# A hybrid decoder block on eight cores: one edit in six parts, from the banks of the attention values to the last multiply

## The chip, the cores and the metric

The kernel runs on all 8 cores of one Trainium2 chip. Each core has one of the 8 batch elements and runs the same program on it, with no exchange between cores. The metric is the device time in microseconds (us) of the slowest core. A core has five engines: PE (TensorE, matrix multiply), DVE (VectorE), ACT (ScalarE), POOL (GpSimd) and SP (SyncE). SP issues most DMAs here and POOL the rest; both run their instructions strictly in order, as the three others do.

## The reference

```python
h = rms_norm(x, norm_mix_pre)                       # (B, 2048, 1024)
u_a, v_a, q, k, v_b, g_a, g_b = split(h @ w_in)     # 7 x 1024 columns
# branch A: chunks of 128 tokens, 8 groups of 128 channels
y_a = gelu(u_a) * (tril(W_s) @ layer_norm(gelu(v_a)) + b_s)
# branch B: 16 heads of 64, three (window, dilation) patterns
for window, dilation in ((128, 1), (512, 4), (2048, 16)):
    o_p, lse_p = causal attention of t on t - j*dilation, j <= window//dilation, ALiBi bias
y_b = sum_p softmax_p(lse_p) * o_p
merged = sigmoid(g_a + b0) * (y_a @ w_a_proj) + sigmoid(g_b + b1) * (y_b @ w_b_proj)
x = x + rms_norm(merged @ w_out, norm_mix_post)
f = square(relu(rms_norm(x, norm_ffn_pre) @ w_ff1)) @ w_ff2      # 1024 -> 4096 -> 1024
x = x + rms_norm(f, norm_ffn_post)
```

## The kernel before

The program is one list of operations, each with the buffers and PSUM banks that it reads and writes. A planner (`Plan.schedule`) gives each operation a cost, and always takes the ready operation of lowest `prio` on the engine that is free first; from that comes a fixed order for every engine. `Plan.emit` writes it out with semaphore waits. So a changed number moves many instructions, and at run time each engine stands at the head of its list until that instruction's waits are met.

The stages, in order of time:

1. **Start.** x is loaded, normed, transposed to `hT`, with the projections of the first heads between.
2. **Attention**, in 8 pairs of heads (`hp` 0 to 7). For a pair, `proj_qk` makes Q and K (8 groups of 8 matmuls of 512 columns, from the pair's weights `wqk`), casts them out of banks 6 and 7 on DVE, and makes two more orders of K: `KT0` by a copy on DVE (L560), `KT1` by a copy on ACT (L562). `s_job` makes scores in banks 0 to 3, ACT takes the exponential to `Et` (L654), DVE multiplies by the bias table to `PT` (L666); there are 8 such jobs of the first pattern and 12 of the others. `pv_class` has four classes `c` in each pair: it gathers all three patterns of a quarter of the tokens, for both heads, in banks 4 and 5, 48 matmuls that alternate between the heads. Then come the logarithm of the sums (L725, ACT, twice), the exponential of that (L727, ACT) and two products into `ybT` (L730, DVE), which free the banks for the next class. The Q and K groups of a pair, and the value projection of pairs of pairs (`proj_v`), stand between the scores and values of the pairs ahead of it, and keep PE at work while it would wait for ACT.
3. **V_A**: 16 tiles of `hT` by `wva`, each in two groups of 8 matmuls. The first 7 (`NRAW`) are made during the last pairs and copied raw (`raw`, L832) because gelu waits for the last exponential of attention (`lastexp`); they alternate in banks 6 and 7. The copies `hTc` are made on POOL (L821).
4. **U**, 8 groups `g` of four (L887 takes gelu), and the **gate products** (`name="gate"`, 4 to a group g, each 4 matmuls of 128 columns), which read all layer-normed V_A tiles `gc` (L852), and which DVE turns into `yaT` (L900, L904). The gate products of group g have the priority of U's group g + 4.
5. **Merge**: for each of 8 blocks and 4 windows four groups (`g0`, `g1` on `hT`, `g3` on `ybT`, `g2` on `yaT`).
6. **Output projection** of 16 token tiles, with norms, the new x stored to `x1_scr`, and `h2T`. The feed-forward layers follow in two halves `s`, each with 7 products in place of 8 (sums and differences of weight blocks, `w1_comb` and `w2_comb`, are made earlier on DVE and stored). The first `NMIX` = 8 groups of half 0's first layer are mixed among the output projections; they use banks 0 and 1 alone. The others take bank pairs in rotation. Their weights come into a ring of 5 buffers (`rslot`; the mixed ones use four of them).
7. **End.** When the 7 products of the second layer are gathered, `fin` makes the factor of each token tile on POOL (L1215, L1217), and DVE multiplies by factor and gain (L1223) and adds x (L1225), half a tile at a time.

The weights of the last pair have a buffer of their own, `wqk2`, on the first 4 KB of `stg[0]`, the staged values of pairs 4 and 5: classes 0 and 1 of pair 5 are the last to read that part. Loads of `wqk` are issued on POOL.

## Time and profile before

| | |
|---|---|
| median of 3 runs | 1166.86 us (lowest 1165.67) |
| the profiled execution | 1166.27 us |
| its slowest core, first to last instruction | 1164.7 us (the eight: 1158.1 to 1164.7) |
| PE busy | 1119.2 us, 96% of the span |
| DVE, ACT, POOL busy | 735.7, 529.0, 149.2 us |
| mean granted TensorE clock | 0.987 |

The profile is of the slowest core. PE's ends are modelled, so one matmul of 512 columns shows about 380 ns though the next one starts 217 ns after it; cadence is to be read from starts. "Busy" PE time thus covers all but true stops. The granted clock is given per stretch, as a share of full speed: 1.00 is 2.4 GHz and 0.50 is 1.2 GHz.

### The profile page before, as it was taken

How to read it: one execution, taken by the hardware profiler on the slowest of the kernel's cores; microseconds unless marked ns; L12 is line 12 of the kernel's file. 1: busy time of each engine (PE TensorE's matmuls, PEld its weight loads, DVE VectorE, ACT ScalarE, POOL GpSimd, SP SyncE). 2: the span in 40 equal slices, each digit the busy share in tenths (PEclk: the TensorE clock that was granted, in tenths of full speed). 3: DMA queues.
4: the chain of work that ended last, by engine and by line, in shares of the span. 5: the costliest groups of instructions: out<-in, count | busy, mean ns of one | idle time of the engine just before them, and what ended most of it. 6: DMA issues, size and time to landing. Idle time of an engine off the chain costs nothing.

```text
span 1164.7 us, 20926 instructions; the slowest of 8 cores (1158.1 to 1164.7 us)
## 1 busy us (share of the span) xinstructions
PE 1119.2 (96%) x7348; PEld 569.9 (49%) x7348; DVE 735.7 (63%) x1224; ACT 529.0 (45%) x771; POOL 149.2 (13%) x260
## 2 busy tenths in 40 slices
PE   8899999997989999999999999999999999999996
PEld 3666665664545445444444444444444444444442
DVE  5867777776777644755444466985783157774417
ACT  4567887787776863021221135653321124432021
POOL 3300000001122441000000012520000031000002
PEclk9899999998999999899999999999999999999999
DMA  8776756676442439389887779975457459547433
GB/s 222 191 180 124 149 117 148 121 146 136 106 69 63 73 63 147 46 179 234 228 215 193 191 250 280 292 255 162 148 170 255 149 182 310 173 155 264 145 113 141
DMA packets 95337, 197.57 MB, mean 170 GB/s; under 512 B 39169, under 2 KB 55681, under 8 KB 90370
## 3 DMA queue, kind: packets, MB, share of 16 engines
q1 hardware_dynamic: 86082, 154.28, 42.6%
q0 software_dynamic: 9152, 41.95, 21.6%
q8 instruction: 61, 1.00, 0.4%
q14 instruction: 42, 0.34, 0.1%
HBM read 194.11 MB, written 56.62 MB: 215 GB/s over the span
## 4 chain that ended last, share of the span: by engine, by line
PE 85%; issue 4%; DVE 4%; ACT 3%; DMA 3%; POOL 1%; DVEq 0%; SPq 0%; ACTq 0%; POOLq 0%
PE pst L195 85%; DMA sb_xt<-x 2%; ACT sb_Et L654 1%; PE pst L199 1%; DVE sb_ybT L730 1%; DMA sb_r<-w_comb 1%; ACT sb_gc L852 0%; DVE sb_PT L666 0%; ACT sb_Lr L725 0%; POOL sb_st L1020 0%; ACT sb_junk L1022 0%; DVE sb_yaT L904 0%; ACT sb_gv L833 0%; ACT sb_Lr L727 0%; DVE sb_tmpm L900 0%
## 5 line engine op out<-in xcount | busy, mean ns | idle before, releaser
L654 ACT ACTIVATE sb_Et<-pst 128x1024 bf16<-128x1024 f32 (+1 forms) x160 | 151.0, 975 | 31.9 <-PE pst L195 16.7
L195 PE MATMUL pst<-sb_r,sb_hid 128*128 128x512 bf16 x640 | 139.4, 379 | 0.3 <-DVE sb_hid L1129 0.3
L666 DVE TENSOR_TENSOR sb_PT<-sb_Et,sb_EB 128x1024 bf16<-128x1024 bf16 (+2 forms) x200 | 110.1, 569 | 36.9 <-ACT sb_Et L654 25.1
L195 PE MATMUL pst<-sb_hT,sb_wqk 128*128 128x512 bf16 x512 | 122.3, 386 | 3.8 <-DVE sb_hT L516 3.1
L965 ACT ACTIVATE sb_sg<-pst,sb_small 128x512 f32<-128x512 f32 x64 | 44.0, 687 | 176.2 <-PE pst L195 71.0
L195 PE MATMUL pst<-sb_merged,sb_r 128*128 128x512 bf16 x512 | 122.2, 379 | 0.5 <-DVE sb_hid L1121 0.5
L195 PE MATMUL pst<-sb_hT,sb_wg 128*128 128x512 bf16 x512 | 116.2, 379 | 0.0
L195 PEld LDWEIGHTS pst<-sb_r,sb_hid 128*128 128x128 bf16 x640 | 62.5, 98 | 76.0 <-issue 0.7
L195 PE MATMUL pst<-sb_TB,sb_r 128*128 128x512 bf16 x384 | 94.1, 379 | 2.8 <-ACT sb_sne L1118 1.7
L195 PEld LDWEIGHTS pst<-sb_merged,sb_r 128*128 128x128 bf16 x512 | 49.8, 98 | 61.1 <-issue 1.8
L195 PEld LDWEIGHTS pst<-sb_hT,sb_wg 128*128 128x128 bf16 x512 | 49.9, 98 | 59.0
L195 PEld LDWEIGHTS pst<-sb_hT,sb_wqk 128*128 128x128 bf16 x512 | 46.9, 99 | 61.2 <-issue 14.6
L1118 ACT ACTIVATE sb_sn<-pst 128x512 f32<-128x512 f32 x72 | 43.0, 597 | 72.6 <-PE pst L195 72.6
L969 DVE SCALAR_TENSOR_TENSOR sb_sg<-sb_sg,pst 128x512 f32<-128x512 f32 x32 | 22.0, 687 | 84.5 <-PE pst L195 84.5
L1205 DVE TENSOR_TENSOR sb_sn<-pst,sb_sn 128x512 f32<-128x512 f32 x24 | 16.4, 690 | 87.6 <-ACT sb_sn L1202 49.5
L195 PE MATMUL pst<-sb_PT,sb_V 128*128 128x64 bf16 (+3 forms) x1280 | 65.0, 209 | 1.5 <-DVE sb_ybT L730 1.4
L195 PE MATMUL pst<-sb_QT,sb_KT 64*128 64x256 bf16 (+1 forms) x768 | 52.5, 250 | 12.7 <-ACT sb_Et L654 12.2
L195 PE MATMUL pst<-sb_ybT,sb_wg 128*128 128x512 bf16 x256 | 62.2, 387 | 1.8 <-DVE sb_tmpm L900 1.8
L195 PEld LDWEIGHTS pst<-sb_PT,sb_V 128*128 128x128 bf16 x1280 | 56.0, 100 | 12.7 <-issue 5.8
L195 PE MATMUL pst<-sb_yaT,sb_wg 128*128 128x512 bf16 x256 | 61.3, 384 | 0.0
L195 PE MATMUL pst<-sb_wout,sb_merged 128*128 128x512 bf16 x256 | 58.5, 379 | 2.5 <-DVE sb_tp L1030 2.5
L195 PEld LDWEIGHTS pst<-sb_TB,sb_r 128*128 128x128 bf16 x384 | 37.2, 98 | 48.2 <-issue 4.4
(123 smaller groups left out, 1668.1 us busy)
## 6 DMA issues: line engine op xcount, KB each, us to landing
w_bf<-w POOLq DMA_DIRECT2D x32, 512.0 KB, 7.8
sb_PB<-w_bf SPq DMA_DIRECT2D x32, 512.0 KB, 8.8
w_comb<-sb_PB SPq DMA_DIRECT2D x32, 512.0 KB, 9.6
sb_r<-w_comb SPq DMA_DIRECT2D x32, 512.0 KB, 4.6
sb_r<-w_comb SPq DMA_DIRECT2D x16, 1024.0 KB, 5.1
sb_r<-w_bf SPq DMA_DIRECT2D x32, 384.0 KB, 3.8
sb_r<-w_bf SPq DMA_DIRECT2D x12, 1024.0 KB, 5.7
...
```

The lines of the kernel that those rows point to most:

```text
L195: e.matmul(out, lhsT=l, rhs=r, start=st, stop=sp, skip_group_check=True))
L199: fns = [lambda e, a=a, b=b: e.transpose(out=a, in_=b, identity=ident) for a, b in outs_ins]
L654: P.act(lambda e: e.activation(out=et[:, :, 0:W], in_=psall[:, sb:sb + 2, 0:W], func=AF.Exp, scale=0.125), 2 * W, [], [et.key()], [sb, sb ...
L666: P.dve(lambda e: e.tensor_tensor(out=o, in0=i0, in1=i1, op=ALU.mult), n, rk, [pt.key()], rate=2, name="mask")
L730: P.dve(lambda e, hh=hh, lo=lo: e.tensor_tensor(out=ybT[lo:lo + 64, hp, 512 * c:512 * c + 512], in0=psr(bks[hh], lo, lo + 64), in1=lr[lo:l ...
L965: P.act(lambda e, j=j, cb=cb, pj=pj, s_=s_: e.activation(out=s_[j][:], in_=pj, func=AF.Tanh, scale=0.5, bias=small[:, bg_c + 8 * j + cb:bg ...
L969: P.dve(lambda e, pj=pj, s_=s_: e.scalar_tensor_tensor(out=s_[1][:], in0=s_[1][:], scalar=1.0, in1=pj, op0=ALU.add, op1=ALU.mult), 512, [s ...
L1118: P.act(lambda e: e.activation(out=o[:], in_=ps(bk), func=AF.Copy), 512, [], [o.key()], [bk], name="snap")
L1205: P.dve(lambda e: e.tensor_tensor(out=d[:], in0=ps(bk), in1=d[:], op=ALU.add), 512, [d.key()], [d.key()], [bk])
```

## The change

Six parts:

1. **PV on three banks.** For pairs 6 and 7 the two heads of a class are written one after the other and no longer alternate, and each takes the next of banks 4, 5 and 7 in turn. The last class still has banks 0 and 1. For that, the raw V_A groups use bank 6 alone.
2. **A home for the last weights.** `wqk2` moves from 64 KB to 60 KB, on the part of `ybT` that pair 7 writes, and its load is placed when pair 5 starts, behind the last class of pair 4. `hTc`'s first four buffers change their order.
3. **K copies on GpSimd.** The 32 copies to `KT1` move from ACT to POOL.
4. **Gate products** of group g get the priority of U's group g + 2.
5. **Six mixed groups** (`NMIX` = 6). The next two of half 0 become groups like the rest; the ring's rule changes with the number.
6. **Final weights ahead of the factor.** `gfin` is multiplied in as soon as a half is gathered and squared, and the factor and the addition of x become one instruction.

```diff
-    wqk.append(buf("wqk2", 64 * K, [8, 256]))
+    wqk.append(buf("wqk2", 60 * K, [8, 256]))
...
-                    c1 = P.act(lambda e, o1=o1, s=s: e.activation(out=o1, in_=s, func=AF.Copy), 512, [kk],
-                               [KT1[d].key((512 * w, 512 * w + 512))])
+                    c1 = P.pool(lambda e, o1=o1, s=s: e.tensor_copy(out=o1, in_=s), 1.2, [kk], [KT1[d].key((512 * w, 512 * w + 512))])
...
-        bks = (0, 1) if hp == NHP - 1 and c == 3 else (4, 5)
+        bks = (4, 5)
+        if hp >= 6:
+            r = [(4, 5, 7)[(pctr3[0] + j) % 3] for j in range(2)]
+            pctr3[0] += 2
+            bks = tuple(r)
+        if hp == NHP - 1 and c == 3:
+            bks = (0, 1)
...
-        for j in range(8):
+        for hs in (((0,), (1,)) if hp >= 6 else ((0, 1),)):
+            bk = [bks[hh] for hh in hs]
+            for j in range(8):
...
-                for hh in range(2):
+                    for hh in hs:
...
-            P.pe(mms, [V0[d].key(), p0t[j].key()], bks, name="pv0")
+                P.pe(mms, [V0[d].key(), p0t[j].key()], bk, name="pv0")
...
-            elif hp == NHP - 2:
-                load_wqk(hp + 1, b0 - 30)
+            elif hp == NHP - 3:
+                load_wqk(hp + 2, b0 - 5, anchor[0])
...
-    hTc = [buf(f"hTc{i}", o * K, [8, 128]) for i, o in enumerate((68, 70, 92, 104, 160, 64, 66, 198, 200, 202))]
+    hTc = [buf(f"hTc{i}", o * K, [8, 128]) for i, o in enumerate((64, 66, 68, 70, 92, 104, 160, 198, 200, 202))]
...
     def vbanks(n):
+        if n < NRAW:
+            return (6, 6)
         return {NRAW: (2, 3)}.get(n, (6, 7))
...
-            P.prio = U0 + 10 * (g + 4) + 5 + n4
+            P.prio = U0 + 10 * (g + 2) + 5 + n4
...
-    NMIX = 8
+    NMIX = 6
...
-                        P.dve(lambda e, src=src, hs=hs: e.scalar_tensor_tensor(out=src, in0=src, scalar=sp_[:, c0 + 3:c0 + 4], in1=gfin[:, hs],
-                                                                              op0=ALU.mult, op1=ALU.mult), 512, [rk, gfin.key()] + k, k, bks)
-                        P.dve(lambda e, src=src, hf=hf, xh=xh: e.tensor_tensor(out=xh(hf), in0=src, in1=xh(hf), op=ALU.add), 512,
-                              [kh[hf]] + k, [kh[hf]], bks)
+                        P.dve(lambda e, src=src, hf=hf, xh=xh: e.scalar_tensor_tensor(out=xh(hf), in0=src, scalar=sp_[:, c0 + 3:c0 + 4], in1=xh(hf),
+                                                                                      op0=ALU.mult, op1=ALU.add), 512, [rk, kh[hf]] + k, [kh[hf]], bks)
...
+                def gain(src, hf, k, bks=()):
+                    P.dve(lambda e: e.tensor_tensor(out=src, in0=src, in1=gfin[:, 512 * hf:512 * hf + 512], op=ALU.mult), 512, k + [gfin.key()], k, bks)
...
                 elif o == 6:
                     acc(u2[p], bk)
                     sq(u2[p][:], 9, [u2[p].key()], [])
+                    gain(u2[p][:], 1, [u2[p].key()])
                     fin(8 * s + p, [(s1[p][:], [s1[p].key()], []), (u2[p][:], [u2[p].key()], [])], 8)
```

Where this moves instructions, three places follow.

PE's list in pair 5, from the last products of class 0 on (`sb_QT_55` is the Q of pair 5, `sb_stgV_48` ends a class, `sb_wqk_64` is `wqk2`). Before:

```order
L195 MATMUL pst<-sb_PT_2_80,sb_stgV_48 128x128 x8
L195 MATMUL pst<-sb_QT_55,sb_KT_57 128x128 x8
L195 MATMUL pst<-sb_QT_55,sb_KT_1_61 128x256 x6
L195 MATMUL pst<-sb_QT_55,sb_KT_1_61 128x128 x2
L195 MATMUL pst<-sb_QT_55,sb_KT_57 128x128 x8
```

and now:

```order
L195 MATMUL pst<-sb_QT_55,sb_KT_57 128x128 x8
L195 MATMUL pst<-sb_PT_2_80,sb_stgV_48 128x128 x8
L195 MATMUL pst<-sb_hT,sb_wqk_64 128x512 x8
L195 MATMUL pst<-sb_QT_55,sb_KT_1_61 128x256 x6
L195 MATMUL pst<-sb_QT_55,sb_KT_1_61 128x128 x2
L195 MATMUL pst<-sb_hT,sb_wqk_64 128x512 x8
L195 MATMUL pst<-sb_QT_55,sb_KT_57 128x128 x8
L195 MATMUL pst<-sb_hT,sb_wqk_64 128x512 x8
```

Q and K of the last pair have moved from pairs 5 (end) and 6 wholly into pair 5. Pair 6 then has 2 groups of V_A as its only other work and pair 7 has 8, where before the V_A groups that stood among both were 12, beside 5 projections.

PE's list at the end of V_A (`sb_wva`), where U (`sb_wu`) and the gate products (`sb_wsT`) follow. Before:

```order
L195 MATMUL pst<-sb_wva,sb_hTc_139 128x512 x16
L195 MATMUL pst<-sb_hT,sb_wu_112 128x512 x16
L195 MATMUL pst<-sb_hT,sb_wu_113 128x512 x24
L195 MATMUL pst<-sb_wsT,sb_gc 128x16x8 x8
L195 MATMUL pst<-sb_hT,sb_wu_114 128x512 x8
```

and now:

```order
L195 MATMUL pst<-sb_wva,sb_hTc_139 128x512 x16
L195 MATMUL pst<-sb_hT,sb_wu_110 128x512 x16
L195 MATMUL pst<-sb_wsT,sb_gc 128x16x8 x8
L195 MATMUL pst<-sb_hT,sb_wu_112 128x512 x8
L195 MATMUL pst<-sb_wsT,sb_gc 128x16x8 x8
```

Two U groups and not five lie between the last V_A group and the first gate products, and 12 gate products and not 20 are left when U ends.

DVE's list at the very end, from the gathering of the last two tiles. Before:

```order
L1205 TENSOR_TENSOR sb_sn_205<-pst,sb_sn_205 128x512
L1205 TENSOR_TENSOR sb_sn_206<-pst,sb_sn_206 128x512
L1223 SCALAR_TENSOR_TENSOR sb_sn_201<-sb_sn_201,sb_st_183,sb_gfin 128x512
L1223 SCALAR_TENSOR_TENSOR sb_sn_205<-sb_sn_205,sb_st_183,sb_gfin 128x512
L1225 TENSOR_TENSOR sb_hx<-sb_sn_201,sb_hx 128x512
L1225 TENSOR_TENSOR sb_hx<-sb_sn_205,sb_hx 128x512
L1223 SCALAR_TENSOR_TENSOR sb_sn_202<-sb_sn_202,sb_st_184,sb_gfin 128x512
L1223 SCALAR_TENSOR_TENSOR sb_sn_206<-sb_sn_206,sb_st_184,sb_gfin 128x512
L1225 TENSOR_TENSOR sb_hx<-sb_sn_202,sb_hx 128x512
L1225 TENSOR_TENSOR sb_hx<-sb_sn_206,sb_hx 128x512
```

and now:

```order
L1242 TENSOR_TENSOR sb_sn_205<-sb_sn_205,sb_gfin 128x512
L1215 TENSOR_TENSOR sb_sn_206<-pst,sb_sn_206 128x512
L1233 SCALAR_TENSOR_TENSOR sb_hx<-sb_sn_201,sb_st_183,sb_hx 128x512
L1233 SCALAR_TENSOR_TENSOR sb_hx<-sb_sn_205,sb_st_183,sb_hx 128x512
L1242 TENSOR_TENSOR sb_sn_206<-sb_sn_206,sb_gfin 128x512
L1233 SCALAR_TENSOR_TENSOR sb_hx<-sb_sn_202,sb_st_184,sb_hx 128x512
L1233 SCALAR_TENSOR_TENSOR sb_hx<-sb_sn_206,sb_st_184,sb_hx 128x512
```

Behind the last gathering (L1215) 5 instructions are left and not 8, and two behind the last factor and not four. In POOL's list the K copies stand between DMA issues: a copy waits there for whatever the issue ahead of it waits for.

## Rows read from the trace of the kernel before

**Rows 1.** Stretches: busy of PE, PEld, DVE, ACT, POOL; granted clock; DMA share; GB/s

```profile
200.00:276.00 76.00, 74.36 (x844) 47.77 (x841) 58.00 (x101) 61.32 (x74) 5.23 (x10) 1.00 0.62 128
276.00:296.00 20.00, 13.11 (x159) 9.59 (x160) 9.83 (x18) 13.19 (x19) 3.08 (x5) 0.74 0.57 119
296.00:325.00 29.00, 27.95 (x254) 14.32 (x253) 22.45 (x38) 24.18 (x28) 3.24 (x4) 1.00 0.49 103
325.00:342.00 17.00, 12.34 (x196) 8.62 (x195) 11.01 (x17) 11.37 (x16) 4.22 (x5) 1.00 0.38 64
...
484.00:492.00 8.00, 5.10 (x21) 1.94 (x20) 4.82 (x10) 0.69 (x1) 0.00 (x0) 0.67 0.00 0
...
777.00:800.00 23.00, 19.85 (x100) 8.50 (x99) 14.02 (x21) 11.66 (x20) 2.22 (x6) 1.00 0.58 189
```

**Rows 2.** PE in order of time: start, us, instructions, idle before and its releaser

```profile
276.35 0.61 PE L195 MATMUL pst<-sb_PT,sb_stgV 128*128 128x128 bf16 x8 [0.46 <-DVE sb_PT L666]
...
279.45 0.34 PE L195 MATMUL pst<-sb_QT,sb_KT 64*128 64x256 bf16 x4 [1.89 <-ACT sb_Et L654]
...
281.57 3.10 PE L195 MATMUL pst<-sb_PT,sb_V 128*128 128x64 bf16 x40 [0.28 <-DVE sb_ybT L730]
...
295.31 3.70 PE L195 MATMUL pst<-sb_hT,sb_wqk 128*128 128x512 bf16 x16
...
338.65 1.85 PE L195 MATMUL pst<-sb_PT,sb_V 128*128 128x64 bf16 x40 [0.20 <-DVE sb_ybT L730]
```

**Rows 3.** POOL in order of time at the load of the last weights

```profile
286.02 0.54 POOL L476 DMA_DIRECT2D sb_wqk<-w_qk  x1 [10.99 <-PE pst L195]
```

**Rows 4.** ACT's groups in 60 to 270 us: busy, mean ns, idle before

```profile
L654 ACT ACTIVATE sb_Et<-pst 128x1024 bf16<-128x1024 f32 x82 | 83.1, 1032 | 20.7 <-PE pst L195 12.8 <-DVE sb_ybT L730 4.0 <-DVE sb_PT L666 3.1
L562 ACT ACTIVATE sb_KT<-sb_KT 128x512 bf16<-128x512 bf16 x25 | 33.8, 1364 | 9.3 <-DVE sb_KT L555 9.3
L725 ACT ACTIVATE sb_Lr<-pst 64x512 f32<-64x512 f32 x40 | 23.7, 592 | 14.4 <-PE pst L195 13.6
L727 ACT ACTIVATE sb_Lr<-sb_Lr 128x512 f32<-128x512 f32 x20 | 12.5, 626 | 0.3
```

**Rows 5.** Waits in 60 to 270 us: total, times, longest

```profile
PE pst L195 <- ACT sb_Et L654: 1.9, 8, 0.5
```

**Rows 6.** POOL's copies of hT: ns min/median/max, first and last start

```profile
L821 POOL COPY sb_hTc<-sb_hT x16: 1026/1044/2019, 287.1 to 422.0; 128x1024 bf16<-128x1024 bf16 x16
```

**Rows 7.** DVE and POOL in order of time at 317 us

```profile
318.49 1.13 DVE L666 TENSOR_TENSOR sb_PT<-sb_Et,sb_EB 128x1024 bf16<-128x1024 bf16 x1 [0.31 <-ACT sb_Et L654]
...
317.00 2.08 POOL L821 COPY sb_hTc<-sb_hT 128x1024 bf16<-128x1024 bf16 x2 [12.26 <-PE pst L195]
```

**Rows 8.** DVE's groups in 60 to 270 us

```profile
L666 DVE TENSOR_TENSOR sb_PT<-sb_Et,sb_EB 128x1024 bf16<-128x1024 bf16 x81 | 54.8, 691 | 14.9 <-ACT sb_Et L654 10.9 <-PE pst L195 2.9
```

**Rows 9.** ACT at the end of V_A, then PE where yaT is waited for

```profile
432.62 0.60 ACT L837 ACTIVATE sb_gv<-pst 128x512 f32<-128x512 f32 x1 [0.98 <-PE pst L195]
...
436.56 1.23 ACT L852 ACTIVATE sb_gc<-sb_gv,sb_bst 128x1024 bf16<-128x1024 f32 x1
...
487.77 3.57 PE L195 MATMUL pst<-sb_ybT,sb_wg 128*128 128x512 bf16 x8 [1.80 <-DVE sb_tmpm L900]
```

**Rows 10.** The end: PE, DVE, then two steps of the chain of waits

```profile
1127.70 26.71 PE L195 MATMUL pst<-sb_r,sb_hid 128*128 128x512 bf16 x123
...
1154.23 1.28 DVE L1205 TENSOR_TENSOR sb_sn<-pst,sb_sn 128x512 f32<-128x512 f32 x2
1157.02 1.42 DVE L1223 SCALAR_TENSOR_TENSOR sb_sn<-sb_sn,sb_st,sb_gfin 128x512 f32<-128x512 f32 x2 [1.50 <-POOL sb_st L1217]
...
1160.88 1.29 DVE L1225 TENSOR_TENSOR sb_hx<-sb_sn,sb_hx 128x512 f32<-128x512 f32 x2
...
1155.02 0.73 ACT sb_junk L1208 x2
...
1156.35 0.57 POOL sb_st L1217
```

More of the change, by code:

```diff
@@ L610, in build_nc @@
     anchor = [None]
+    pctr3 = [0]
     sctr, p0ctr, p12ctr, ectr, lctr = [0], [0], [0], [0], [0]
@@ L705, in pv_class @@
-        for n2 in range(2):
-            mms = []
-            for m in (2 * n2, 2 * n2 + 1):
-                w = 64 if m < 3 else 32
-                for hh in range(2):
-                    r = p1t[n2][:, hh, 256 * (m % 2):256 * (m % 2) + 4 * w]
-                    mms.append((out(hh, 0, 4, 32 * m, w), lhs(V1[d], 4 * c + m, hh), r.rearrange("p (a m) -> p a m", a=4), False, False,
-                                4 * w, False))
-            P.pe(mms, [V1[d].key(), p1t[n2].key()], bks, name="pv1")
@@ L714, in pv_class @@
[L714 to L719 removed]
+        for hs in (((0,), (1,)) if hp >= 6 else ((0, 1),)):
+            bk = [bks[hh] for hh in hs]
+            for j in range(8):
+                mms = []
+                for blk in (2 * j, 2 * j + 1):
+                    w = 16 if blk < 15 else 8
+                    for hh in hs:
+                        r = p0t[j][:, hh, 256 * (blk % 2) + 4 * w * c:256 * (blk % 2) + 4 * w * c + 4 * w]
+                        mms.append((out(hh, 0, 4, 8 * blk, w), lhs(V0[d], blk, hh), r.rearrange("p (a m) -> p a m", a=4), first[hh], False,
+                                    4 * w, False))
+                        first[hh] = False
+                P.pe(mms, [V0[d].key(), p0t[j].key()], bk, name="pv0")
+            for n2 in range(2):
+                mms = []
+                for m in (2 * n2, 2 * n2 + 1):
+                    w = 64 if m < 3 else 32
+                    for hh in hs:
+                        r = p1t[n2][:, hh, 256 * (m % 2):256 * (m % 2) + 4 * w]
+                        mms.append((out(hh, 0, 4, 32 * m, w), lhs(V1[d], 4 * c + m, hh), r.rearrange("p (a m) -> p a m", a=4), False, False,
+                                    4 * w, False))
+                P.pe(mms, [V1[d].key(), p1t[n2].key()], bk, name="pv1")
+            mms = []
+            for a in range(4):
+                for hh in hs:
+                    mms.append((ps(bks[hh])[:, 128 * a:128 * a + 128], stg[sd][:, 4 * c + a, hj, 64 * hh:64 * hh + 128],
+                                p2t[:, hh, 128 * a:128 * a + 128], False, a == 3, 128, False))
+            anchor[0] = P.pe(mms, [stg[sd].key((4 * c, 4 * c + 4)), p2t.key()], bk, name="pv2")
@@ L1237, in build_nc @@
                     sq(s1[p][:], 8, [s1[p].key()], [])
+                    gain(s1[p][:], 0, [s1[p].key()])
                 elif o == 3:
```

14 lines of the change are left out of this document (2 added, 12 removed).

## The prediction

> **What bounds the kernel now.** The page says that PE is busy for 96% of the span, so I went first to the stretches in which it is not. The table of stretches [rows 1] shows where PE's share falls: 6.9 us idle of 20 from 276 to 296, 1.0 of 29 to 325, 4.7 of 17 to 342, 2.9 of 8 from 484 to 492 and 3.2 of 23 from 777 to 800. Add the end, in which PE has stopped, about 10 us after its last matmul at 1154.4 [rows 10]. The second thing in that table is the granted clock: 0.74 in the first of these stretches and 0.67 in the fourth. A matmul group shows both levels. 40 products of values take 3.10 us after the idle time at 281 and 1.85 us at 338 [rows 2]; 8 matmuls of 512 columns take 3.57 us at 487 [rows 9], where the usual pace is 26.71 / 123 = 0.217 us each, 1.74 us [rows 10]. So after a stop PE runs for a while at 1.2 GHz and not at 2.4. Everywhere else PE is full at clock 1.00, and there an edit can only lose. From 200 to 276 it is idle for 1.6 us in 76.
>
> So the prize is small and can be counted: about 13 us of idle and 3.4 us of slow clock (13.11 busy us at 0.74) around the last pairs, 4.6 us at 484, 3 us at 777, and some of the end.
>
> **Last weights and three banks.** Why does PE stop at 276? The projections of pair 7 are its filler, and their weights are issued only at 286.02, having waited for PE [rows 3], since their place was still read by pair 5; the first products follow at 295.31 [rows 2]. In between PE has only scores and values, and waits for ACT. With the new place the load can go behind pair 4's last class, a class, some 11 us, ahead of class 0 of pair 5, whose last values ended at 277.0 (276.35 + 0.61) [rows 2], so near 266. Load to first use was 9.3 us, so the weights are there by 275.5, and PE's new list wants them behind class 0 of pair 5, whose end that is. I count no wait for them, with 1.5 us to spare.
>
> But filler is moved, not made. All 8 groups (8 x 1.74 = 13.9 us) now stand in pair 5, and pair 6 has only 2 V_A groups. A class of pair 6 asks PE for 1.85 + 0.6 us of values and five score jobs of some 0.3 us [rows 2], 3.9 us, and 0.9 us of V_A. It asks ACT for five exponentials (1.03, the smaller ones less), two logarithms of 0.59 and one of 0.63 [rows 4], 6.7 us. With two banks a class cannot be faster than its own loop either: values, logarithms, exponential, two products, values again: 1.85 of values, 3 x 0.6 for ACT's steps [rows 4], and DVE's products of about that length with the hand-overs between, some 7 us at full clock (an estimate), and 1.25 more of values at slow clock [rows 2], 8.3. Three banks let the first head of a class start before the last class is cleared; ACT's 6.7 us stay. So in pair 6 PE idles 6.7 - 4.8 = 1.9 us a class, 7.6 us in all. Pair 7 has 8 V_A groups, 3.9 - 0.6 + 3.5 = 6.8 us of PE a class against some 4.8 of ACT (three exponentials), so PE is the longer; one bank for V_A makes each of its groups wait for a copy, for which I leave 3 us. Before: 12.6 + 3.4 = 16.0 us. Now: 7.6 + 3 = 10.6 us. **Gain 5 us.** Bounds: if pair 6 goes round in 8.3 us like the slow loop, 4 x 1.6 = 6.4 us more for the loop and some 1.6 of slow clock are lost, -3 us; if ACT's work spreads so that pair 6 has 2 us of idle, +11. I take 5, because the stretch from 325 to 342, at 73% busy, kept clock 1.00 and is the nearest thing to the new pair 6.
>
> **K copies.** On ACT a copy takes 1.36 us [rows 4], 32 x 1.36 = 44 us of ACT. But PE waited for an exponential only 1.9 us in 60 to 270 [rows 5], so off the path nearly all of it buys nothing there; in pairs 5 to 7 it is already counted, as my 6.7 us have no copy in them. POOL's price for this copy stands nowhere; a copy of twice the elements takes 1.04 us and at most 2.02 [rows 6], so 0.5 to 2.0 us, against a deadline a head pair later. It costs DVE something: a bias multiply that met two POOL copies took 1.13 us [rows 7] against 0.69 [rows 8]. 32 x 0.44 = 14 us of DVE, which has 18 of 76 us free from 200 to 276 [rows 1]. **Gain 1 us**; bounds -3 (some of DVE's delay reaches the banks that PE wants) and +2 (the waits for exponentials go).
>
> **Gate products.** Before, DVE ended the last `yaT` late and PE lost 2.9 us idle and 3.57 - 1.74 = 1.8 us at slow clock [rows 1, 9]. With 12 products and not 20 behind U, and a merge group between each two, DVE keeps pace, and this goes: 4.7 us. What is late next is the other end. The second gate product needs the norm of the last V_A tile, which ended at 436.56 + 1.23 = 437.8, 5.2 us after the last gelu of V_A began at 432.62 [rows 9]. Only two U groups, 3.5 us, and one gate product now lie in between: PE waits 1.5 us, and may have a short slow stretch after it. **Gain 2.5 us**, bounds 0.5 and 4.7.
>
> **Six mixed groups.** 3.2 us were lost behind the output projections, where the last mixed groups share banks 0 and 1 [rows 1]. Groups 6 and 7 now take bank pairs in turn. But group 6 gets the ring buffer of group 5, so its load cannot start until group 5 is done, as group 8's could not behind group 7 before. **Gain 1.5 us**, bounds -2 and +3.
>
> **The end.** Before, the last sums are gathered at 1154.23 to 1155.5, the first factor arrives at 1157.0, and 8 instructions follow, to 1162.2 [rows 10]. Now the gatherings of the first three tiles are no longer held up. PE's end at 1154.4 stays. Then one gathering 0.7, one square 0.8, the two steps on POOL 1.1 with their gaps, and two last multiplies 1.4: 1154.5 + 0.7 + 0.8 + 1.2 + 1.4 = 1158.6; the gain multiply runs beside POOL, but the third tile's two multiplies stand ahead of it and may push by 0.2. **Gain 3.4 us**, bounds 2.5 and 3.8. The last store follows as before. The two halves' earlier ends have as many DVE instructions as before and PE is full there: nothing.
>
> **Sum.** 5 + 1 + 2.5 + 1.5 + 3.4 = 13.4 us. 1166.27 - 13.4 = 1152.9 for a profiled execution; the median of runs was 0.6 above that one, 1153.5 us. All lower bounds together give a loss of 1 us, all upper ones a gain of 24.5.
>
> **A rule of the skill that speaks against it.** The trace shows the two at once: POOL's pair of copies at 317.00 and a bias multiply that took 0.44 us longer [rows 7, 8]. The Trainium skill (SBUF — State Buffer, "SBUF: two separate sides") says that DVE instructions with two SBUF inputs and GpSimd instructions that read SBUF take turns on one pair of ports, the first one holding it to its end while the other waits in full. The trace agrees as far as it goes, and by that rule a multiply can wait a whole copy.
>
> **Rivals.**
> *K copies slow the path* (slower than before). The mechanism: every copy stands in POOL's list among DMA issues that wait for a class of the pair ahead, and each holds DVE up. If a copy lasts 2 us and each of some three multiplies that meet it waits, DVE gets 28 x 2 = 56 us more over 240 us, 53 + 16 of each 70: it is full, PE starts to wait for casts and multiplies, and slow clock comes with that, about 4 us for each of 6 pairs. Total 1153.5 + 24 + 1 = 1178. It decides from about 1.5 us of DVE lost per copy; the one meeting in the trace cost 0.44. Chance 0.06, a third of it above the 2% line.
> *Pair 6 starves.* The idle and the slow clock of 276 to 296 move into pair 6, over four classes and not two. The stage then gains between -3 and 0. For: pair 6 has less filler than any pair before. Against: the 73% stretch. Time 1153.5 + 5 to 8, 1158.5 to 1161.5. Chance 0.25.
> *All holes close.* The loop was the limit and not ACT, the gate wait is hidden, the mixed groups flow: 11 + 2 + 4.5 + 3 + 3.6 = 24 at most, likely 18 to 22, so 1145 to 1149. Chance 0.14.
> *The list doesn't fit the chip.* The planner's idea of the loads is short of what they take; one new wait, on `wqk2`, on the ring or on the norm, eats 6 to 8 us: 1160 to 1165. The change then moves holes and doesn't close them. Chance 0.07.
> My forecast, 1149.5 to 1158, has 0.48.
>
> **Range and chances.** From 1145 to 1163 the range holds the forecast, the starved pair, nearly all of the closed holes and half of the last rival. A measurement of this kernel tells about 2% from no change, and that is 1143.5 and 1190.2. Every mechanism that I can name for a gain ends at some 24 us, so faster by over 2% has 0.04; the slow side has 0.02; within 2% has 0.94.
>
> **What would show it.** In the new trace: the load of `wqk2` issued near 266 and no PE wait for a DMA behind it; PE full and clock 1.00 from 276 to 300; a stretch after 300 in which PE is 70% busy and ACT nearly full; no wait for `tmpm` before the first `yaT` products, but one of 1 to 2 us ahead of the second gate product; `KT` copies of about 1 us on POOL; 4 to 5 us from PE's last matmul to DVE's last instruction, where there were 7.8. I am wrong if pair 6 shows clock under 0.9, if bias multiplies in the middle pairs lengthen past 0.8 us on average, or if the feed-forward part has a new wait.

## The result and the profile after

The changed kernel takes 1149.64 us (median of 4 runs, 1148.66 to 1151.09); the kernel before takes 1166.86 us on the same chip (median of 3 runs, 1165.67 to 1171.77). The ratio is 0.9847, 95% interval 0.9827 to 0.9866: 17 to 18 us less. Some executions of most of these kernels come out 30 to 200 us longer, with one die's cores at a lower clock, and they are left out of every time and ratio here. The profiled execution took 1150.46 us, its slowest core (5) 1148.6 us from first to last instruction, against 1166.27 and 1164.7 before: 15.8 us less. The forecast was 1153.5 us, a gain of 13.4.

The stretches of [rows 1], in the changed kernel. The stretch from 764 holds the output projections and the last mixed groups, which stood at 777 before:

```profile
276.00:296.00 20.00, 18.22 (x192) 9.91 (x191) 17.93 (x27) 11.54 (x15) 10.06 (x9) 1.00 0.54 114
296.00:325.00 29.00, 25.53 (x339) 15.88 (x337) 22.39 (x38) 25.10 (x33) 4.68 (x6) 1.00 0.65 122
325.00:342.00 17.00, 16.14 (x188) 8.88 (x184) 15.29 (x25) 14.62 (x18) 6.13 (x8) 1.00 0.68 94
484.00:492.00 8.00, 8.00 (x38) 3.63 (x37) 3.42 (x8) 2.06 (x3) 1.07 (x2) 1.00 0.24 70
764.00:787.00 23.00, 21.06 (x109) 9.56 (x107) 14.41 (x21) 11.69 (x21) 2.22 (x6) 1.00 0.54 186
```

From 276 to 342 PE is idle for 6.1 us where it was for 12.6, and the granted clock is 1.00 throughout. The hole at 484 is gone: in the whole of 345 to 480, where the same matmuls now stand, some 14 us earlier, PE is idle for 0.6 us. Of the 3.2 us idle of the mixed groups 1.9 are left.

The last weights: their issue on POOL, and PE's first product with them, which answer to [rows 2, 3]:

```profile
265.32 0.57 POOL L476 DMA_DIRECT2D sb_wqk<-w_qk  x1 [2.20 <-PE pst L195]
...
279.73 1.89 PE L195 MATMUL pst<-sb_hT,sb_wqk 128*128 128x512 bf16 x8 [1.46 <-DMA sb_wqk<-w_qk]
```

The issue is at 265.3, as forecast, but the weights come after 14.4 us and not 9.3, and PE waits 1.46 us. On core 6 it waits 2.2, on core 0 0.5, on the other five not visibly.

The end, which answers to [rows 10]: PE, DVE, ScalarE and GpSimd in order of time.

```profile
1129.77 8.80 PE L195 MATMUL pst<-sb_r,sb_hid 128*128 128x512 bf16 x40
...
1138.68 0.69 DVE L1215 TENSOR_TENSOR sb_sn<-pst,sb_sn 128x512 f32<-128x512 f32 x1 [0.30 <-PE pst L195]
...
1142.26 1.41 DVE L1233 SCALAR_TENSOR_TENSOR sb_hx<-sb_sn,sb_st,sb_hx 128x512 f32<-128x512 f32 x2 [0.97 <-POOL sb_st L1227]
...
1139.46 0.63 ACT L1218 ACTIVATE sb_junk<-sb_sn 128x512 bf16<-128x512 f32 x1 [2.73 <-DVE sb_sn L1215]
...
1141.52 0.56 POOL L1227 TENSOR_TENSOR sb_st<-sb_st,sb_nhalf 128x1 f32<-128x1 f32 x1
```

DVE's last instruction ends at 1142.26 + 1.41 = 1143.67, 5.1 us behind PE (7.8 before). But the span ends at 1148.6, 4.9 us behind DVE, where it was 1164.7 - 1162.2 = 2.5. From PE's last matmul to the end it is 10.0 us against 10.3: almost nothing was won at the end.

Where the 16.1 us of span between the two slowest cores lie: 13.7 up to the first product of the mixed groups (728.42 before, 714.76 now), 2.2 from there to PE's last matmul, 0.3 behind it.

### The profile page after: what moved, and what is told of

It is laid out like the page before. It is cut to its first block, busy times and chain, and to the rows that moved or that the text cites. A ratio compares the mean times of both kernels' runs of the same rounds, so it can differ in the third digit from the quotient of the medians.

```text
span 1148.6 us, 21017 instructions; the slowest of 8 cores (1142.3 to 1148.6 us)
## 1 busy us (share of the span) xinstructions
PE 1114.1 (97%) x7348; PEld 567.5 (49%) x7348; DVE 747.6 (65%) x1224; ACT 492.4 (43%) x739; POOL 205.5 (18%) x292
## 4 chain that ended last, share of the span: by engine, by line
PE 90%; DMA 3%; DVE 2%; issue 2%; ACT 1%; POOL 1%; SPq 0%; DVEq 0%; POOLq 0%; ACTq 0%
PE pst L195 89%; DMA sb_wqk<-w_qk 1%; DMA sb_xt<-x 1%; PE pst L199 1%; DVE sb_PT L666 1%; ACT sb_Et L654 1%; DMA sb_r<-w_bf 0%; DVE sb_tp L1040 0%; ACT sb_junk L1032 0%; POOL sb_st L1030 0%; DVE sb_xo L1042 0%; DVE sb_ybT L738 0%; DVE sb_raw L842 0%; SPq L498 0%; DVE sb_xn L1047 0%
## 5 line engine op out<-in xcount | busy, mean ns | idle before, releaser
L666 DVE TENSOR_TENSOR sb_PT<-sb_Et,sb_EB 128x1024 bf16<-128x1024 bf16 (+2 forms) x200 | 121.9, 634 | 21.1 <-ACT sb_Et L654 14.7
L1128 ACT ACTIVATE sb_sn<-pst 128x512 f32<-128x512 f32 x78 | 46.4, 597 | 77.2 <-PE pst L195 77.2
L195 PEld LDWEIGHTS pst<-sb_hT,sb_wqk 128*128 128x128 bf16 x512 | 47.1, 99 | 59.1 <-issue 12.6
L562 POOL COPY sb_KT<-sb_KT 128x512 bf16<-128x512 bf16 x32 | 52.4, 1658 | 120.9 <-DVE sb_KT L555 113.8
L1225 POOL TENSOR_SCALAR sb_st<-sb_st 128x1 f32<-128x1 f32 x16 | 9.3, 583 | 335.4 <-ACT sb_junk L1218 335.3
L1215 DVE TENSOR_TENSOR sb_sn<-pst,sb_sn 128x512 f32<-128x512 f32 x24 | 16.6, 690 | 81.1 <-ACT sb_sn L1212 47.1
```

Of the source, the lines that this page charges most:

```text
L195: e.matmul(out, lhsT=l, rhs=r, start=st, stop=sp, skip_group_check=True))
L562: c1 = P.pool(lambda e, o1=o1, s=s: e.tensor_copy(out=o1, in_=s), 1.2, [kk], [KT1[d].key((512 * w, 512 * w + 512))])
L666: P.dve(lambda e: e.tensor_tensor(out=o, in0=i0, in1=i1, op=ALU.mult), n, rk, [pt.key()], rate=2, name="mask")
L1128: P.act(lambda e: e.activation(out=o[:], in_=ps(bk), func=AF.Copy), 512, [], [o.key()], [bk], name="snap")
L1215: P.dve(lambda e: e.tensor_tensor(out=d[:], in0=ps(bk), in1=d[:], op=ALU.add), 512, [d.key()], [d.key()], [bk])
L1225: P.pool(lambda e: e.tensor_scalar(out=sp_[:, c0 + 2:c0 + 3], in0=sp_[:, c0:c0 + 1], scalar1=sp_[:, c0 + 1:c0 + 2], scalar2=DM * EPS, op0= ...
```

## The experiments

Cores differ by up to 6 us inside one execution, by small stalls. So besides the ratio of times each kernel is read by medians over its eight cores: **stage**, the time from PE's first score product (at 61 to 65 us) to the first product of the mixed feed-forward groups (near 710), which holds attention, V_A, U and the gates; and PE's idle time in three stretches, 262 to 300, 300 to 345 and 345 to 480 us. Each is worked out from the eight cores' rows. Four kernels in the table run the same instructions up to the mixed groups (changed, c_after, e3 and e4), and their stages are 647.2 to 649.4 us; three more do with one load earlier (e8, t1 and t2), and theirs are 646.5 to 647.4. A difference of 1 or 2 us between two single executions is therefore not much.

| kernel | ratio to before, 95% | stage, us | idle, us |
|---|---|---|---|
| before | 1 | 662.0 | 7.7, 5.7, 1.5 |
| changed | 0.9847, 0.9827 to 0.9866 | 648.0 | 2.3, 4.4, 0.4 |
| c_after | 0.9862, 0.9824 to 0.9900 | 649.4 | 2.1, 4.5, 0.6 |
| e1_kact | 0.9936, 0.9923 to 0.9950 | 656.7 | 5.1, 7.2, 0.5 |
| e2_gates4 | 0.9905, 0.9884 to 0.9925 | 652.0 | 2.3, 4.2, 3.1 |
| e3_mix8 | 0.9877, 0.9859 to 0.9895 | 647.2 | 2.4, 4.5, 0.2 |
| e4_tail | 0.9860, 0.9842 to 0.9878 | 647.3 | 2.5, 4.3, 0.2 |
| e5_twobanks | 0.9898, 0.9870 to 0.9925 | 654.0 | 2.0, 5.8, 5.7 |
| e6_wqkold | 0.9907, 0.9888 to 0.9926 | 654.8 | 8.0, 2.4, 0.3 |
| e8_early | 0.9846, 0.9820 to 0.9871 | 647.0 | 2.3, 4.3, 0.2 |
| e9_early_kact | 0.9870, 0.9832 to 0.9909 | 649.6 | 2.3, 5.9, 0.2 |
| b1_home | 1.0058, 1.0039 to 1.0077 | 667.6 | 4.6, 7.8, 6.1 |
| t1_nofactor | 0.9827, 0.9807 to 0.9847 | 646.5 | 2.3, 4.1, 0.2 |
| t2_actfactor | 0.9825, 0.9803 to 0.9847 | 647.4 | 2.2, 4.4, 0.2 |

e1 to e4 shared a chip, c_after, e5, e8 and e9 another, e6, b1 and t1 a third, and t2 had a fourth.

### e1_kact: the K copies back on ACT

```diff
-c1 = P.pool(lambda e, o1=o1, s=s: e.tensor_copy(out=o1, in_=s), 1.2, ...)
+c1 = P.act(lambda e, o1=o1, s=s: e.activation(out=o1, in_=s, func=AF.Copy), 512, ...)
```

> The changed kernel with one part undone: the 32 K copies back on ACT. Theory A (the copies are off the path; in the changed kernel they cost DVE about 1 us for each bias multiply that meets one, and buy ACT time that nobody waited for): the time stays within 2 us of the changed kernel, 1148 to 1152; in 60 to 276 us PE's idle time falls by up to 1.5 us, the longest bias multiply goes from 1.7 us back to 0.7, and in 276 to 345 PE's idle grows by no more than 2 us. Rival B (the copies are what freed ACT for the last pairs): PE's idle from 276 to 345, about 6 us in the changed kernel, grows to 10 or more, 1154 to 1158.

1158.29 us, 9.4 us more in the stage than e3 and e4 beside it. As a number that is rival B, but not by its cause. Core 7 of this kernel, the last weights' issue on POOL and PE's first product with them:

```profile
264.48 0.57 POOL L476 DMA_DIRECT2D sb_wqk<-w_qk  x1 [8.75 <-PE pst L195]
...
280.05 3.57 PE L195 MATMUL pst<-sb_hT,sb_wqk 128*128 128x512 bf16 x8 [6.21 <-DMA sb_wqk<-w_qk]
```

PE now asks for the weights 280.05 - 6.21 - 264.48 = 9.4 us after their issue, in the changed kernel 279.73 - 1.46 - 265.32 = 12.9: with the copies on ACT the list has them wanted 3.5 us sooner. They still take 15.6 us, PE waits 6.2 and then runs eight matmuls at half clock (3.57 us). Five cores wait 4.0 to 6.2 us. The other three (0, 3, 6) have no such wait and end at 1143 to 1145 us, the five at 1154 to 1157. So both theories missed: what the copies' engine decided here was whether a load came in time.

### e2_gates4: gate products four U groups behind

```diff
-P.prio = U0 + 10 * (g + 2) + 5 + n4
+P.prio = U0 + 10 * (g + 4) + 5 + n4
```

> The changed kernel with the gate products four U groups behind again, 20 and not 12 of them behind U. Theory A (the whole stall at tmpm was the number of gate products behind U): the wait for tmpm comes back with its slow stretch, 2.9 idle and 1.8 of slow clock, and nothing is regained at the last V_A tile, since no wait is seen there now: 4 to 5 us more, 1153.5 to 1155. Rival B (the stall was bound to the place of V_A and the banks, and has gone with the new order of V_A): no wait for tmpm over 1 us, within 1 us of the changed kernel.

1153.19 us; stage 4.8 us longer than in e3 and e4, theory A. The stall is back on core 0, at the same matmuls as in [rows 9]:

```profile
472.18 0.38 PE L195 MATMUL pst<-sb_wsT,sb_gc 128*128 128x128 bf16 x4 [0.80 <-DVE sb_tmpm L910]
472.83 0.38 PE L195 MATMUL pst<-sb_wsT,sb_gc 128*128 128x128 bf16 x4 [0.28 <-DVE sb_tmpm L910]
```

followed by one of 1.80 us. So the whole 4.7 us was the number of gate products behind U, and nothing is paid for it at the other end.

### e3_mix8: eight mixed groups

```diff
-NMIX = 6
+NMIX = 8
```

> The changed kernel with eight mixed groups again. Theory A (as PE's rows from the first output projection to the end say, 475.6 us before and 473.5 now): 2 us more, from the waits for sne, hid and the combined weights at the end of the mixed groups, 1151.5 to 1153; the stretch from the first wout product to PE's last matmul goes from 473.5 back to 475.6. Rival B (those 2 us are chance, such as the combined weights landing late in that one run of before): the stretch stays at 473.5 within 0.5.

1151.04 us. From the first mixed product to PE's last matmul the quickest core takes 424.87 us, the quickest core of before also 424.87, and those of all kernels with six groups 423.22 to 423.24; the medians of this run and of e4 are 425.30 and 423.23. So the part is worth 1.65 us on an undisturbed core, theory A, a little less than its 2 us.

### e4_tail: the old end

```diff
-scalar_tensor_tensor(out=xh(hf), in0=src, scalar=factor, in1=xh(hf), op0=mult, op1=add)
+scalar_tensor_tensor(out=src, in0=src, scalar=factor, in1=gfin[:, hs], op0=mult, op1=mult)
+tensor_tensor(out=xh(hf), in0=src, in1=xh(hf), op=add)
```

and the `gain` multiplies are gone.

> The changed kernel with the old multiply by factor and weights and the old add at the end. Between PE's last matmul and DVE's last instruction lie 5.1 us now and lay 7.8 before, but from there to the end of the span 4.9 us and 2.5. Theory A (the last 2.4 us belong to the shorter end: something else, not the stores, ends about 10 us after PE and takes over): the stretch from DVE's end to the span's end goes back to 2.5, and the time stays within 0.5 us of the changed kernel. Rival B (the 2.4 us are from another part of the change, and the tail's gain is real): DVE ends 7.8 us after PE, the span 4.9 after that, 2.7 us more than the changed kernel, 1152.3.

1148.84 us, and the span ends 2.56 us behind DVE (up to 2.71 on two cores): theory A. PE to the end is 10.18 us, in the changed kernel 10.05. The new tail gains 0.1 us. What ends there in its place is found by t1 and t2.

### c_after, e8_early: the changed kernel, and the last weights one pair earlier

> The changed kernel itself once more, beside the next three on one chip. All theories: 0.985 of the kernel before, within 0.002; on the cores that end last PE waits 0.5 to 2.3 us for the wqk2 load near 277, as four of the eight cores' traces did before or nearly.

```diff
-elif hp == NHP - 3:
-    load_wqk(hp + 2, b0 - 5, anchor[0])
+if hp == NHP - 4:
+    load_wqk(hp + 3, b0 + 20, anchor[0])
```

The place is `ybT`'s last eighth, free until pair 7 writes it, so nothing forbids it.

> The changed kernel with the last weights loaded one pair earlier still, into the same place. PE's order is the same row for row. Theory A (the load takes 14 to 16 us from issue on the cores where it meets other transfers, and the wait of up to 2.2 us for it sets which core ends last): no wait for that load on any core, the cores' spans draw together, 1.5 to 3 us less than the changed kernel. Rival B (the slow cores are slow for another reason and the wait just shows there): the wait goes but the median falls by under 1 us.

c_after: 1150.27 us, 0.9862. (The profiled execution, at 1157.24, is the longest of its four; the others are at 1150.2 to 1150.3.) In the profile only core 7 waits for the weights, 3.75 us, with the slow clock behind it. The core that ended last (0, at 1155.4) had another stall (last section), so the expectation that the wait decides the last core held only in part. e8_early: 1150.08 us, the load is issued at 220.4 and PE waits for it on no core, as theory A says. The first mixed product comes at 707.4 to 711.5 over the cores, in c_after at 707.7 to 719.3, in the changed kernel's other profile at 709.1 to 715.0. But the time falls by 0.2 us alone, less than the 1 us under which rival B puts it, and the ratio (0.9846) is that of the changed kernel in its first measurement (0.9847). Over the seven profiles the mean stage is 1.1 us shorter with the early load (646.9 and 648.0). So the wait is gone, and what it was worth in time, theory A's 1.5 to 3 us, is not shown.

### e9_early_kact: the early load, and the copies on ACT

> The early load, with the K copies on ACT. With the copies on ACT and the load at its new time the kernel took 9 us more, and the traces show 4 to 6.2 us of wait for that load on five cores and a slow clock behind it, while the other three were as fast as the changed kernel. Theory A (that wait was all, the engine of the copies is nearly nothing): within 2 us of the early load with the copies on GpSimd. Rival B (ACT's 44 us for the copies also hold the path in the last pairs): 4 us or more above it, in 296 to 345 us.

Stage 649.6, 2.6 us more than e8_early and 2.2 to 3.1 more than the three kernels with the early load. The time is 1152.0 us against 1150.08, 1.9 us more (the intervals of the ratios overlap). PE's list is that of e1, row for row. The load's wait is gone on all cores, and with it 7 of the 9.4 us of e1. What is left lies where rival B says, 300 to 345: 5.9 us of idle against 4.3, and clock 0.92 to 0.96 on the eight cores against 1.00 on seven of eight. So the copies' engine is worth 1.9 us by time, inside theory A's 2, and 2.6 by stage, between the two theories.

### e5_twobanks: two banks for the last values

```diff
-if hp >= 6:                                  # three banks, head by head
+if False:
-for hs in (((0,), (1,)) if hp >= 6 else ((0, 1),)):
+for hs in ((0, 1),):
-    if n < NRAW: return (6, 6)
```

> The changed kernel with two banks for the values of pairs 6 and 7, both heads at once, and two banks for V_A; the new place and time of the last weights kept. Theory A (most of the 10 us of the attention stage come from the earlier weights, the third bank gives 2 to 3): 1149.5 to 1151 on the scale on which the changed kernel has 1147; PE's idle from 296 to 345 grows from 4.3 to 6 or 8 us. Rival B (the third bank is what keeps pair 6 full): idle over 10 us with slow clock, 1155 or more. Rival C (one bank for V_A costs what the third gives): no change within 1 us.

1156.11 us, 5.8 us over c_after, and the stage 4.6 us. Two stretches of its slowest core, then of the changed kernel's:

```profile
300.00:345.00 45.00, 39.24 (x485) 1.00 0.53 101
345.00:480.00 135.00, 129.35 (x838) 0.99 0.53 74
```

```profile
300.00:345.00 45.00, 40.68 (x520) 1.00 0.64 108
345.00:480.00 135.00, 134.40 (x831) 1.00 0.57 82
```

(The columns: us, PE busy, clock, DMA share, GB/s.) Between the theories in size, and elsewhere than either had it: pair 6 loses 1.4 us, and 5 us go behind 345, most of them in one wait behind the last values:

```profile
367.96 2.47 PE L195 MATMUL pst<-sb_hT,sb_wu 128*128 128x512 bf16 x8 [3.46 <-DVE sb_ybT L738]
```

The first U group waits there for the last `ybT`, and runs at reduced clock behind it. So the edit (third bank, values head by head, one bank for V_A, which were not taken apart) pays at the end of pair 7, not where the prediction looked for it.

### e6_wqkold: the last weights in the old place

```diff
-wqk.append(buf("wqk2", 60 * K, [8, 256]))
+wqk.append(buf("wqk2", 64 * K, [8, 256]))
-elif hp == NHP - 3: load_wqk(hp + 2, b0 - 5, anchor[0])
+elif hp == NHP - 2: load_wqk(hp + 1, b0 - 30)
```

and the old order of the `hTc` places.

> The changed kernel with the last weights back in their old place and loaded at their old time; three banks for the values, K copies on GpSimd and the rest kept. Theory A (the hole of 276 to 296, 7 us of idle and 3.4 of slow clock, was the missing filler, as the prediction has it): the hole comes back, clock under 0.9 in 262 to 300, 7 us or more above the changed kernel, with pair 6 fuller in exchange for at most 3. Theory B (the sum of the parts undone so far leaves the new place nearly nothing: gate products 5.3, banks 3.8, copies 3.4, of 12.6 us up to the first merged product): within 3 us of the changed kernel, as three banks alone would fill the hole.

1154.26 us, stage 654.8, which is 5.4 to 7.6 us over the four executions with the new place. Its slowest core:

```profile
262.00:300.00 38.00, 29.52 (x324) 0.82 0.71 121
300.00:345.00 45.00, 41.82 (x484) 1.00 0.56 91
```

The hole is back, 8.5 us idle at clock 0.82, and from 300 to 345 PE idles 2.4 us (median) and not 4.4: theory A in kind, at the lower end of its 7 us or more.

### b1_home: the new place alone, on the kernel before

The edit is that of e6_wqkold the other way round, in the kernel before.

> The kernel before with the new place and load time of the last weights alone. Theory A (filler is what was missing): the hole at 276 closes, clock 0.95 or more in 262 to 300, and some of it opens again in pair 6 with two banks and the K copies on ScalarE: 4 to 8 us less than before. Theory B (filler is only moved): within 2 us of the kernel before; the idle time of 262 to 300 turns up in 300 to 345, from 5.7 us to over 11.

1172.57 us: **slower** than before, by 0.58% with an interval that excludes no change, which neither theory had. Five cores wait for the weights, 3.2 to 7.5 us. Core 6:

```profile
281.51 3.57 PE L195 MATMUL pst<-sb_hT,sb_wqk 128*128 128x512 bf16 x8 [7.54 <-DMA sb_wqk<-w_qk]
```

Core 1, which did not have to wait:

```profile
262.00:300.00 38.00, 37.03 (x384) 1.00 0.58 116
300.00:345.00 45.00, 37.51 (x439) 0.92 0.55 102
345.00:480.00 135.00, 128.61 (x816) 0.99 0.52 82
```

There the hole at 276 is closed, and 7.5 and 6.4 us of idle stand behind it: filler (matmuls that keep PE at work while the scores wait for ACT) moved, not made, as theory B says, on a core without the wait. With the wait it is a loss.

### t1_nofactor, t2_actfactor: what ends the program

t1, on e8_early: the last tile is scaled by the factor of the tile ahead, and its two GpSimd steps are left out.

> The early load's kernel with the last tile scaled by the factor of the tile ahead of it: the two GpSimd steps of the last tile are left out, so that tile is not normed by its own sum. DVE's last instruction comes some 2.4 us earlier, about 2.7 us behind PE's last matmul. So far the span has ended 4.9 us behind DVE's last instruction with the new tail and 2.5 with the old, and about 10 us behind PE's last matmul with both. Theory A (something at the end counts from PE's or ScalarE's last work): the span still ends 10 us behind PE. Theory B (it counts from GpSimd's last instruction, 6.5 us behind it with the new tail): 6.1 to 6.5 us behind the last GpSimd step that is left, which is 3.9 us earlier, so 6 to 7 us behind PE unless the stores' 2.5 us behind DVE end later. Theory C (a fixed 4.9 us behind DVE for this form of the tail): 7.6 us behind PE.

Over the eight cores, median: DVE 4.05 us behind PE, the span's end 2.44 behind DVE and 6.48 behind PE. Theories A (10) and C (7.6) fall. Held against GpSimd's last instruction, all kernels with the factor on GpSimd agree, old tail or new (medians, us):

| | DVE behind PE | end behind DVE | end behind PE | end behind GpSimd |
|---|---|---|---|---|
| before | 7.75 | 2.56 | 10.32 | 6.54 |
| e4_tail (old tail) | 7.62 | 2.56 | 10.18 | 6.54 |
| changed | 5.10 | 4.95 | 10.05 | 6.54 |
| e8_early | 5.10 | 4.95 | 10.05 | 6.53 |
| t1_nofactor | 4.05 | 2.44 | 6.48 | 6.86 |
| t2_actfactor | 4.05 | 2.42 | 6.47 | 6.85 |

The other eight executions lie at 6.53 or 6.54 too. The trace names what fills that time. Each engine's list closes with an instruction DRAIN, on line 341, where the block of all engines ends; it doesn't count as busy time. GpSimd's and SyncE's in the slowest core of before, then of the changed kernel, then of t2 (count: shortest/median/longest in ns, start of the first and last in us):

```profile
L341 POOLq DRAIN  x1: 7174/7174/7174, 1157.3 to 1157.3; - x1
L341 SPq DRAIN  x1: 7/7/7, 1164.5 to 1164.5; - x1
```

```profile
L341 POOLq DRAIN  x1: 6897/6897/6897, 1141.5 to 1141.5; - x1
L341 SPq DRAIN  x1: 7/7/7, 1145.9 to 1145.9; - x1
```

```profile
L341 POOLq DRAIN  x1: 7109/7109/7109, 1135.8 to 1135.8; - x1
L341 SPq DRAIN  x1: 7/7/7, 1143.2 to 1143.2; - x1
```

GpSimd's DRAIN ends 6.30 to 6.31 us behind GpSimd's last instruction on every core of all fourteen executions, t1 and t2 too. SyncE's ends 0.08 us behind the landing of the last store. The span ends 0.21 to 0.23 us behind whichever of the two ends later, again on all 112 cores. Before, both ended at 1164.5; the new tail shortened only SyncE's, by 2.4 us. In t2 SyncE's is the later one.

t2 keeps the whole computation. The last factor is made on ScalarE (the two new instructions, in short):

```diff
+P.act(Ln:  st[c0+3] = ln(st[c0+1] + st[c0+2]))      # st[c0+2] = first half's sum + eps, long ready
+P.act(Exp: st[c0+3] = exp(-0.5 * st[c0+3]))
```

for the last tile alone, with one `Ln` at the start of the last gatherings.

> The whole computation again, on top of the early load: only the last tile's factor is made on ScalarE and not on GpSimd, as exp(-0.5 ln(sum)) behind its square, with one such logarithm far ahead so that the functions are there. Theory A (what held the end was GpSimd's last instruction, 6.5 us ahead of the end of the span at the least; without it the end follows DVE by 2.5 us, as in the run without the factor): DVE's last instruction 4.0 to 4.6 us behind PE's last matmul, the end of the span 2.5 us behind that, 6.5 to 7.1 behind PE where the changed kernel has 10.0, so 3 us less than the early load alone: 0.982 of the kernel before. Theory B (the end shortened because no factor was waited for, whoever makes it): 4.9 us behind DVE again, 0.984 or more. Theory C (ScalarE loads its functions anew behind the square): DVE's last instruction over 5.5 us behind PE.

Core 3, the slowest (span 1143.4), DVE, ScalarE and GpSimd:

```profile
1139.61 1.41 DVE L1242 SCALAR_TENSOR_TENSOR sb_hx<-sb_sn,sb_st,sb_hx 128x512 f32<-128x512 f32 x2
...
1138.68 0.29 ACT L1229 ACTIVATE sb_st<-sb_st 128x1 f32<-128x1 f32 x1
1139.06 0.20 ACT L1231 ACTIVATE sb_st<-sb_st 128x1 f32<-128x1 f32 x1
...
1135.82 0.77 POOL L1236 TENSOR_TENSOR sb_st<-sb_st,sb_nhalf 128x1 f32<-128x1 f32 x1
```

GpSimd is done at 1136.6, the factor at 1139.3, DVE at 1141.0, and the span at 1143.4: 6.47 us behind PE (median) where the changed kernel has 10.05, theory A. 1146.02 us, 0.9825, beats both kernels: 20 us under before, and 3.6 us under the changed kernel by the rows of its end. GpSimd's DRAIN is still only 0.3 us ahead of SyncE's, so taking still more off GpSimd alone would win nothing here. (The interval of its ratio, 0.9803 to 0.9847, still touches that of the changed kernel.)

## Why the prediction was right, and where it was not

**The sum.** Forecast 13.4, measured 15.8 between the profiled executions. The sign, the places and the bound ("every gain ends at some 24 us") held. The terms stand otherwise, so that the total came within 2.4 us is in part luck: their errors have both signs.

| term | forecast | measured | from |
|---|---|---|---|
| weights, three banks, K copies | 5 + 1 | 9.2 | 662.0 - 648.0, less the gates' 4.8 |
| gate products | 2.5 | 4.8 | e2 |
| six mixed groups | 1.5 | 1.65 | e3 |
| the end | 3.4 | 0.1 to 0.3 | e4 |

They add to 15.8 to 16.0. The first is what is left of the stage, and as the same program's stage is 647.2 to 649.4 in four executions it is known to about 1 us. Two terms were too small by 5.5 together, one too large by 3.2. One sum of the prediction is wrong as a sum: its lower bounds, -3 - 3 + 0.5 - 2 + 2.5, give a loss of 5 us and not 1; nothing came near them.

"Everywhere else PE is full" is wrong too, though no term hangs on it. The first 60 us of the kernel before:

```profile
0.00:30.00 30.00, 24.35 (x128) 11.33 (x129) 16.60 (x18) 13.56 (x22) 11.13 (x24) 1.00 0.89 225
30.00:60.00 30.00, 26.45 (x208) 17.94 (x206) 23.68 (x30) 16.90 (x25) 11.31 (x18) 0.89 0.69 187
```

9.2 us of idle and some slow clock stand there, in no part of the change.

**Weights and banks.** The step "in pair 6 PE idles 6.7 - 4.8 = 1.9 us a class" failed on its second number. 26 us of pair 6, 304 to 330, about four classes (the last values of pair 5 are done at 308.5 and those of pair 6 at 333.5; that stretch of 25 us has 3.1 us of idle):

```profile
304.00:330.00 26.00, 22.53 (x309) 13.91 (x310) 20.12 (x36) 24.88 (x33) 3.35 (x5) 1.00 0.73 136
```

ACT is busy for 6.2 us a class (6.7 forecast) and nearly full, as said; PE is for 5.6 and not 4.8, so it idles 0.9 a class. Half of the difference is V_A: 24 of its products fell into this stretch (and into that of 25 us), 1.3 us a class and not 0.9. The rest is in scores and values, and was not taken apart. Also, the 3 us left for V_A's single bank were not paid: PE waited 0.7 us in all for `sb_raw`. The change needs its parts together. Taking one out costs 4.6 us (banks), 5 to 8 (place) or 9.4 (copies, most of it the wait for the load that e1 brings), more than the 9.2 in all; the place alone on the old kernel loses. So a term for each part, added up, was the wrong form: each part only closes a hole that the others don't open again elsewhere.

**The load** was costed at "load to first use was 9.3 us, ... with 1.5 us to spare". 9.3 was the time from issue to first use in the trace of before, and not what the load took. From issue to landing, in the slowest core of before and of the changed kernel:

```profile
DMA to landing us min/median/max: 5.6/5.6/5.6
```

```profile
DMA to landing us min/median/max: 14.3/14.3/14.3
```

Over the eight cores it was 5.0 to 7.2 us before, with one to three other loads in flight, and 8.3 to 15.1 us in the changed kernel, with seven or eight. The company is not all of it: with the same seven, three cores had 8.3 to 8.6 and one 12.2. Of the rivals, "a new wait on `wqk2`" named it, at 6 to 8 us; in the changed kernel and its relatives with this load time (c_after, e2 to e5) it costs 0.1 to 3.8 us on some cores, and e1 and b1, in which the list asks for the weights some 3.5 us sooner, show 3.2 to 7.5 us.

**K copies.** The range for the price on GpSimd held: 1.66 us (median), 1.33 to 2.01, in 0.5 to 2.0; "about 1 us", named as a sign, did not. The groups and one meeting at 295 us, POOL and DVE in order of time:

```profile
L562 POOL COPY sb_KT<-sb_KT x32: 1330/1662/2007, 53.8 to 300.4; 128x512 bf16<-128x512 bf16 x32
```

```profile
294.85 1.91 POOL L562 COPY sb_KT<-sb_KT 128x512 bf16<-128x512 bf16 x1 [2.48 <-DVE sb_KT L555]
...
295.36 1.70 DVE L666 TENSOR_TENSOR sb_PT<-sb_Et,sb_EB 128x1024 bf16<-128x1024 bf16 x1
```

The multiply takes 1.70 us where [rows 8] have 0.69, so it lost 1.0 us, more than the 0.44 us that the prediction had from before, and it ends 0.3 us behind the copy. In 60 to 270 us eight of the 82 such multiplies take over 1 us, 1.05 to 1.71. Each of them meets a copy that began ahead of it, and each ends 0.28 to 0.31 us behind that copy's end. The rule of the Trainium skill (SBUF — State Buffer, "SBUF: two separate sides") has the later one wait for the whole of the other. The trace agrees in kind; in size it is less, since a multiply that ran wholly behind the copy would end 0.69 us behind it.

Over the middle pairs, 60 to 270 us, DVE's group of those multiplies that answers to [rows 8]:

```profile
L666 DVE TENSOR_TENSOR sb_PT<-sb_Et,sb_EB 128x1024 bf16<-128x1024 bf16 x82 | 61.7, 770 | 8.4 <-ACT sb_Et L654 4.4 <-PE pst L195 3.2
```

0.77 us on average against 0.69, 6.5 us of DVE in 210: under the 0.8 that the prediction named as its mark, and far from the rival's 1.5 us per copy, as most copies meet no such multiply. What the copies gave was 1.9 us by time and 2.6 by stage (e9 against e8; forecast 1, bound 2), in 300 to 345, where ACT is nearly full.

**Gate products.** The gain at the far end was whole, 4.8 us. The forecast took 1.5 to 2.2 us off for a wait ahead of the second gate product, and that wait doesn't exist. ACT at the last V_A tile, then PE, where 8 matmuls are a pair of gate products:

```profile
420.44 1.23 ACT L862 ACTIVATE sb_gc<-sb_gv,sb_bst 128x1024 bf16<-128x1024 f32 x1
...
419.69 0.61 PE L195 MATMUL pst<-sb_wsT,sb_gc 128*128 128x128 bf16 x8
420.14 1.89 PE L195 MATMUL pst<-sb_hT,sb_wu 128*128 128x512 bf16 x8
421.86 0.61 PE L195 MATMUL pst<-sb_wsT,sb_gc 128*128 128x128 bf16 x8
```

The norm ends at 421.67, the second pair starts at 421.86, and its second product, which reads the last tile, 0.2 us later. The forecast counted two U groups and one gate product behind the last V_A; there is a third U group (420.14) between the two pairs. It stands in the order's rows ahead of the prediction, and was missed in the sum. The margin is 0.2 to 0.4 us.

**Mixed groups.** Right, 1.65 of 1.5.

**The end.** "4 to 5 us from PE's last matmul to DVE's last instruction" measured 5.1. What failed is "the last store follows as before": it assumed that the store was what ended the span. The rows of before allowed the other reading. GpSimd's last one there:

```profile
1157.35 0.84 POOL L1217 TENSOR_TENSOR sb_st<-sb_st,sb_nhalf 128x1 f32<-128x1 f32 x1
```

It ends at 1158.2, 6.5 us before the span does. And the DRAIN rows of before (shown with t1) have GpSimd's end at 1157.3 + 7.2 = 1164.5, where SyncE's also stands: two ends within 0.1 us of each other, of which the change shortened one. The prediction's rows did not have them.
